# A decoder step with product-key experts: 72 instead of 64 tokens weighed from gathered expert rows, with a third place for the rows and half of each group's rows sent one group ahead

## The chip, the cores and the metric

The kernel runs as one program on one core of a Trainium2 chip. The metric is the device time of one execution in microseconds (us). TensorE (PE) multiplies, VectorE (DVE) and ScalarE (ACT) prepare its operands, GpSimd (POOL) issues the indirect DMAs (gathers and scatters), and SyncE (SP) issues the plain loads. The engines have their own instruction streams and meet at semaphores.

## The reference, cut to what matters

288 tokens (256 of a prompt, 32 of eight samples) go through a mixer stage (short convolution and sparse attention) and then through a product-key expert stage with 128 x 128 = 16384 experts. The change touches only the expert stage:

```
qq = (hx @ wq).reshape(pb, PEER_HEADS, 2, PEER_HALF)
s = jnp.einsum('nhcd,hckd->nhck', qq, sub_keys)
...                      # top 16 of the pair sums for each of 8 heads: 128 experts a token
g = jax.nn.softmax(top, axis=-1)
a = jax.nn.gelu(jnp.einsum('nd,nhkd->nhk', hx, u_tab[eidx]), approximate=False)
w = (g * a).astype(hx.dtype)
return jnp.einsum('nhk,nhkd->nd', w, v_tab[eidx])
```

So every token picks 128 of 16384 experts, and its output is a weighted sum of 128 rows of `v_tab`, each 1024 wide.

## The kernel before, in words

**Dense, in float32 by parts.** The expert stage does not look experts up for most tokens: it multiplies all 16384 rows of both tables with the tokens, and sets the weights of unpicked experts to zero. A table is cut into 128 tiles of 128 x 1024. A tile comes in through a ring of four slots (SP, L534 and L541); ACT writes its rounded part `w_hi` (L974), DVE the rest `w_lo` (L1445), and PE multiplies both.

**U stage** (L2168 and L2173, 128 tiles): 24 matmuls a tile, each with all 288 tokens as moving columns. The activations of the dense tokens stay in SBUF (`rows`), those of the gathered tokens (the last `NE`) are stored to DRAM (`act_kept`, L522).

**Routing.** The gates of the first 128 tokens reach the dense weights through DRAM: POOL scatters them (L607), SP loads them back in 32 pieces of 512 columns into four buffers `gates_in` (L530), DVE multiplies them in (`weighed`). The dense tokens from 128 to `ND` are routed on PE in groups of four (`route`, L2222, four matmuls a group), one group at every second U tile from tile 71. There are `GROUPS = (ND - 128) / 4` of them, 24 before.

**V stage** (`value_tile`, L2248 and L2255, 128 tiles): eight matmuls a tile with `w_hi` and `2 * ND` moving columns (the rounded part and the rest of the weights side by side), then eight with `w_lo` and `ND` columns. The moving operands are made by ACT (L1042) and DVE (L1666).

**Gathered tokens.** For the last `NE` tokens the picked rows of V are fetched: one indirect DMA (L617, issued by POOL) fetches for one token the 128 half rows of 512 values, one on each partition, 256 KB. The tokens go in `EGROUPS` groups of four. A group is a unit of two halves (`weigh_unit`, L2286): a half is four fp32 matmuls with 512 moving columns, each with its own 32 columns of the array, and it needs the four gathered rows of that half and the four tokens' weights (L1719), for which POOL gathers the activations from DRAM (L624). The units stand ahead of the V tiles `UNIT_TILES`, so PE's order is written out: the two halves of a unit, then six or seven tiles, then the next unit. There are two places for rows, one for each half; POOL may fetch into a place when the half before it is done (`rows_used`). POOL's order is written out too: `at_tile(t)` waits until V tile `t - 1` is done, and spreads the issues over the tiles. At V tile `SUM_AT` ACT copies the summed units out of PSUM (L1076), and before tile 126 PE turns them (L2295).

Of the kernel before, what the change touches and what calls it, by code (L numbers as in the profile page):

```python
# [47 lines left out]
NE = 64  # L48
# [3 lines left out]
UNIT_TILES = [13 + 7 * g for g in range(EGROUPS)]  # L52
SUM_AT = UNIT_TILES[-1] + 2
STAGE = 4
# [50 lines left out]
UP0 = 17904  # L105
# [13 lines left out]
assert UP0 + RT["sp"][0] <= AR_ROWS and AR["vset"][0] <= AR_ROWS and RT["ab"][0] + GRP * P == RT["abf"][1] and 4 * ND <= 2 * GRP * P  # L119
assert AR_ROWS + (HOTS + 1) * P + ND - P <= min(UP0 + RT["ab"][0], AR["vset"][1])  # L120
MOVES = 3
assert GATES + D <= AUX and 4 * NT + 4 * ND <= KC * NT - P
assert GATES + 2 * PIECE * P <= AUX and AR_ROWS + 2 * GRP * 512 + 2 * PIECE * P <= AR_STAGE
# [96 lines left out]

def v_tile(t):
    pp, dh = t % HALF, t // HALF
    return pp // 32 * 64 + dh * 32 + pp % 32


def program(nc, A, O):
    with ExitStack() as ctx:
# [20 lines left out]
        e_sums, e_ident = aux[:, GATES:GATES + D], h2_over[:, KC * NT - P:KC * NT]  # L248
# [14 lines left out]
        gates_in += [arena[:, x:x + PIECE * P] for x in (AR_ROWS + 2 * GRP * 512, AR_ROWS + 2 * GRP * 512 + PIECE * P)]  # L263
# [23 lines left out]
        at = AR_ROWS - AR["vset"][0]  # L287
# [3 lines left out]
        g_hi, g_lo = hots[:, HOTS, 0:ND - P], arena[:, AR_ROWS + (HOTS + 1) * P:AR_ROWS + (HOTS + 1) * P + ND - P]  # L291
# [8 lines left out]
        e_rows = [arena[:, AR_ROWS + i * GRP * 512:AR_ROWS + (i + 1) * GRP * 512] for i in range(2)]  # L300
# [255 lines left out]
        def _(pool):  # L556
# [57 lines left out]
            def gather_row(k, q):  # L614

                n = ND + GRP * (k // 2) + q
                pool.indirect_dma_start(e_rows[k % 2][:, 512 * q:512 * q + 512], None, A["v"].rearrange("t p (c f) -> (t p c) f", f=512),  # L617
                                        bass.IndirectOffsetOnAxis(row_list[:, n:n + 1], 0), element_offset=(k % 2) * 32 * P * D)\
                    .then_inc(S[f"v_in{k % 2}"], 16)
# [21 lines left out]
            for n in range(2 * GRP):  # L641
                at_tile(3 + n)
                gather_value(n // GRP, n % GRP)
            for g in range(1, EGROUPS):
                T = UNIT_TILES[g - 1]
                if g >= 2:
                    pool.wait_ge(S["s_weights"], 2 + g - 1)
                for half in range(2):
                    pool.wait_ge(S["rows_used"], 2 * (g - 1) + half + 1)
                    gather_row(2 * g + half, 0)  # L650
                gather_row(2 * g, 1)
                at_tile(T + 1)
                gather_row(2 * g + 1, 1)
                next_value(g, 0)
                at_tile(T + 2)
                gather_row(2 * g, 2)
                next_value(g, 1)
                at_tile(T + 3)
                gather_row(2 * g + 1, 2)
                next_value(g, 2)  # L660
                at_tile(T + 4)
                gather_row(2 * g, 3)
                gather_row(2 * g + 1, 3)
                at_tile(T + 5)
                next_value(g, 3)
# [1064 lines left out]
        def _(pe):  # L1730
# [547 lines left out]
            def weigh_unit(k):  # L2278

                g, half = k // 2, k % 2  # L2280
                pe.wait_ge(S[f"v_in{half}"], 16 * 9 * SETB + 16 * GRP * (g + 1))
                if half == 0:
                    pe.wait_ge(S["s_weights"], 2 + g + 1)
                for q in range(GRP):
                    at = 31 + 32 * (GRP * g + q) - g
                    last = pe.matmul(ps[32 * q:32 * q + 32, 6 + half, :], e_wide[:, at:at + 32], e_rows[half][:, 512 * q:512 * q + 512],  # L2286
                                     start=(g == 0), stop=(g == EGROUPS - 1), skip_group_check=True)
# [152 lines left out]
```

## Time and profile before

| | us |
|---|---|
| three runs | 1204.32, 1205.97, 1201.17 (median 1204.32) |
| profiled execution, its own time | 1203.3 |
| its span in the profile | 1201.6 |
| PE busy | 1170.2 (97%) |
| DVE busy | 848.6 (71%) |
| ACT busy | 624.7 (52%) |
| POOL busy | 574.6 (48%) |
| bytes moved by DMA | 263.67 MB, 219 GB/s over the span |

PE is busy nearly all of the span, at a mean granted clock of 0.99. Busy time of a PE instruction overlaps with the next one's, so the pace of PE is read from the distance between starts, not from the mean duration of an instruction. `PEld` is the load of a matmul's stationary operand, which the profile lists by itself.

### The profile page before, as it was taken

Reading aid. Unit: us, or ns where it says so; the run is one execution under the profiler, and the core shown is the slowest. Engines: PE = TensorE matmul, PEld = TensorE weight load, DVE = VectorE, ACT = ScalarE, POOL = GpSimd, SP = SyncE. Lnnn points to the kernel's source line nnn. Section 1 sums busy time; section 2 is a strip of 40 time slices with the busy share of each in tenths; the row PEclk is TensorE's granted clock in tenths of the full one; section 3 lists DMA queues with packets and bytes.
Section 4 is the critical chain, followed back from the end, with each engine's and each line's share of the span. In section 5 each row is a group of like instructions: output and inputs, shape, how many; then the busy total and the mean of one; then the engine's idle time right before and its main releaser. Section 6 shows DMA issues by size and latency. Waiting matters only on the chain.

```text
span 1201.6 us, 23451 instructions
## 1 busy us (share of the span) xinstructions
PE 1170.2 (97%) x8260; PEld 1080.2 (90%) x8260; DVE 848.6 (71%) x1593; ACT 624.7 (52%) x1209; POOL 574.6 (48%) x525
## 2 busy tenths in 40 slices
PE   7999899979999999999999999999999999999998
PEld 5688899957799999999999999999988988788888
DVE  6536465736587699999967788896966666656665
ACT  5424464523254454554556777765655555555554
POOL 3430324542000088777778776203365656565640
PEclk9999998989999999999999999999999999999999
DMA  8673437866675357677776666689888888889883
GB/s 323 208 225 103 127 94 229 277 211 236 170 275 177 105 176 176 167 171 184 171 186 168 154 165 171 201 247 334 319 286 298 290 297 284 279 275 308 287 293 128
DMA packets 140197, 263.67 MB, mean 219 GB/s; under 512 B 50992, under 2 KB 79728, under 8 KB 139376
## 3 DMA queue, kind: packets, MB, share of 16 engines
q1 hardware_dynamic: 100176, 207.29, 52.7%
q0 software_dynamic: 37184, 51.48, 17.3%
q10 hardware_dynamic: 2720, 3.40, 0.8%
q8 instruction: 66, 1.08, 0.3%
q14 instruction: 51, 0.42, 0.1%
HBM read 246.18 MB, written 20.09 MB: 222 GB/s over the span
## 4 chain that ended last, share of the span: by engine, by line
PE 84%; issue 5%; DMA 2%; POOL 2%; POOLq 2%; DVE 2%; SPq 1%; ACT 1%; ACTq 0%; DVEq 0%
PE ps L2168 27%; PE ps L2248 16%; PE ps L2173 13%; PE ps L2255 9%; PE ps L1735 5%; PE ps L2286 2%; PE ps L1882 2%; PE ps L1755 2%; POOLq L571 1%; DMA arena<-in_v,aux 1%; PE ps L2222 1%; POOL arena L572 1%; PE ps L1851 1%; PE ps L1844 1%; PE ps L1762 1%
## 5 line engine op out<-in xcount | busy, mean ns | idle before, releaser
L974 ACT ACTIVATE w_hi<-ring 128x1024 fp32r<-128x1024 f32 x280 | 296.9, 1060 | 333.0 <-issue 258.2
L1445 DVE TENSOR_TENSOR w_lo<-ring,w_hi 128x1024 fp32r<-128x1024 f32 x271 | 331.2, 1223 | 169.0 <-ACT w_hi L974 167.4
L2168 PE MATMUL ps<-h_hi,w_hi 128*128 128x288 f32 x1088 | 294.6, 299 | 0.5 <-ACT w_hi L974 0.5
L2168 PE MATMUL ps<-h_lo,w_hi 128*128 128x288 f32 x1024 | 277.0, 295 | 0.0
L607 POOL DMA_INDIRECT gates<-arena x128 | 243.9, 1906 | 68.3 <-issue 47.0
L617 POOL DMA_INDIRECT arena<-in_v,aux x128 | 135.2, 1057 | 155.0 <-PE ps L2286 63.4
L2168 PEld LDWEIGHTS ps<-h_hi,w_hi 128*128 128x128 f32 x1088 | 205.1, 188 | 1.2 <-ACT w_hi L974 1.0
L2168 PEld LDWEIGHTS ps<-h_lo,w_hi 128*128 128x128 f32 x1024 | 192.4, 188 | 0.0
L2173 PE MATMUL ps<-h_hi,w_lo 128*128 128x288 f32 x1088 | 167.3, 296 | 0.2 <-DVE w_lo L1445 0.2
L2248 PE MATMUL ps<-h_hi,w_hi 128*128 128x448 f32 x680 | 154.0, 368 | 0.9 <-DVE h_hi L1666 0.5
L2173 PEld LDWEIGHTS ps<-h_hi,w_lo 128*128 128x128 f32 x1088 | 151.7, 188 | 0.5 <-DVE w_lo L1445 0.5
L2248 PEld LDWEIGHTS ps<-h_hi,w_hi 128*128 128x128 f32 x680 | 121.4, 189 | 18.4 <-issue 9.9
L2255 PEld LDWEIGHTS ps<-h_hi,w_lo 128*128 128x128 f32 x680 | 89.1, 191 | 2.4
L2255 PE MATMUL ps<-h_hi,w_lo 128*128 128x224 f32 x680 | 89.1, 273 | 0.0
L624 POOL DMA_INDIRECT arena<-act_kept,aux x64 | 65.0, 1016 | 49.4 <-PE ps L2255 33.2
L597 POOL TENSOR_TENSOR w_lo<-ring,w_hi 128x1024 fp32r<-128x1024 f32 x9 | 24.6, 2731 | 133.1 <-ACT w_hi L974 133.1
L2248 PE MATMUL ps<-mov,w_hi 128*128 128x448 f32 x344 | 77.7, 368 | 0.0
L2248 PEld LDWEIGHTS ps<-mov,w_hi 128*128 128x128 f32 x344 | 61.5, 189 | 8.2 <-issue 4.2
L572 POOL DMA_DIRECT2D arena<-in_cache_slc_v x64 | 34.8, 544 | 61.0 <-issue 61.0
L1666 DVE TENSOR_TENSOR h_hi<-arena,h_hi 128x448 fp32r<-128x448 f32 x85 | 52.5, 618 | 0.6 <-ACT h_hi L1042 0.6
L1042 ACT ACTIVATE h_hi<-arena 128x448 fp32r<-128x448 f32 x85 | 47.7, 562 | 1.0 <-DVE arena L1650 1.0
L1735 PE MATMUL ps<-xT,ring 128*128 128x288 f32 x192 | 47.9, 408 | 0.0
(367 smaller groups left out, 1928.3 us busy)
## 6 DMA issues: line engine op xcount, KB each, us to landing
ring<-in_uT SPq DMA_DIRECT2D x128, 512.0 KB, 3.4
ring<-in_v SPq DMA_DIRECT2D x128, 512.0 KB, 4.5
ring<-in_wout SPq DMA_DIRECT2D x32, 512.0 KB, 4.4
ring<-in_wT SPq DMA_DIRECT2D x28, 512.0 KB, 4.3
gates<-aux SPq DMA_DIRECT2D x32, 256.0 KB, 6.0
ring<-in_wtok SPq DMA_DIRECT2D x8, 512.0 KB, 4.9
arena<-in_cache_slc_v POOLq DMA_DIRECT2D x64, 64.0 KB, 3.9
act_kept<-arena SPq DMA_DIRECT2D x32, 128.0 KB, 3.8
```

Source lines behind the costliest of these rows:

```text
L607: pool.indirect_dma_start(gates, bass.IndirectOffsetOnAxis(rt("gi")[:, P + s:P + s + 1].bitcast(U32), 0), rt("gi")[:, s:s + 1], None, comp ...
L617: pool.indirect_dma_start(e_rows[k % 2][:, 512 * q:512 * q + 512], None, A["v"].rearrange("t p (c f) -> (t p c) f", f=512), bass.IndirectO ...
L624: pool.indirect_dma_start(e_act[:, n:n + 1], None, act_kept, bass.IndirectOffsetOnAxis(act_list[:, ND + n:ND + n + 1], 0))\
L974: act.activation(w_hi[e % 2][:, :], ring[:, (W_O + e) % RING, :], ACT.Copy).then_inc(S["w_high"], 1)
L1042: act.activation(mov_parts[t % MOVES][:, :, 0, :], rows[:, 2 * pp:2 * pp + 2, :], ACT.Copy).then_inc(S["mov_high"], 1)
L1445: dve.tensor_tensor(w_lo[e % 2][:, :], ring[:, (W_O + e) % RING, :], w_hi[e % 2][:, :].bitcast(F32), ALU.subtract)\
L1666: dve.tensor_tensor(mov_parts[t % MOVES][:, :, 1, :], rows[:, 2 * pp:2 * pp + 2, :], mov_parts[t % MOVES][:, :, 0, :].bitcast(F32), ALU.su ...
L1735: last = pe.matmul(ps[:, bank, 0:NT], ring[:, i % RING, at + k * P:at + (k + 1) * P], rhs[:, k, :], start=(k == 0), stop=(k == n - 1))
L2168: last = pe.matmul(ps[:, bank, 0:NT], w_hi[e % 2][:, k * P:(k + 1) * P], mov[:, k, :], start=(k == 0 and mov is mov_hi), stop=False, skip_ ...
L2173: last = pe.matmul(ps[:, bank, 0:NT], w_lo[e % 2][:, k * P:(k + 1) * P], mov_hi[:, k, :], start=False, stop=(k == KC - 1), skip_group_chec ...
L2248: last = pe.matmul(ps[:, VBANK[dh][m], 0:2 * ND], w_hi[e % 2][:, h * 512 + m * P:h * 512 + (m + 1) * P], both[h], start=(t % HALF == 0 and ...
L2255: last = pe.matmul(ps[:, VBANK[dh][m], 0:ND], w_lo[e % 2][:, h * 512 + m * P:h * 512 + (m + 1) * P], both[h][:, 0:ND], start=False, stop=( ...
```

## The change

`NE` goes from 64 to 72, so `ND` from 224 to 216 and `GROUPS` from 24 to 22; there are 18 gathered groups instead of 16. The units stand at V tiles 10, 17, 23, 30, 36, 43, 50, 56, 63, 70, 76, 83, 89, 96, 103, 109, 116, 123 instead of 13, 20, ..., 118, so 11 of the 17 distances are seven tiles and six are six tiles; `SUM_AT` goes from 120 to 125. The four buffers `gates_in` become a third place for gathered rows once all 32 pieces are weighed. Half number `k` (two for each group) uses place `k` for the first two and then `(k - 2) % 3`. Of each group's rows, those of the first half are sent one group earlier than before. Several regions of the arena move; the sums are copied into the arena instead of `aux`.

```diff
-NE = 64
+NE = 72
...
-UNIT_TILES = [13 + 7 * g for g in range(EGROUPS)]
+UNIT_TILES = [10] + [17 + 106 * g // (EGROUPS - 2) for g in range(EGROUPS - 1)]
 SUM_AT = UNIT_TILES[-1] + 2
+PLACES = 3
...
+def row_place(k):
+
+    return k if k < 2 else (k - 2) % PLACES
+
+
+def row_uses(k):
+
+    return len([x for x in range(k + 1) if row_place(x) == row_place(k)])
...
+        e_rows.append(gates_in)
+        e_sums = arena[:, AR_ROWS:AR_ROWS + D]
+        row_sems = [("v_in0", 16 * 9 * SETB), ("v_in1", 16 * 9 * SETB), ("k_in0_0", 16 * 4 * 2)]
...
             for n in range(2 * GRP):
-                at_tile(3 + n)
+                if n >= GRP:
+                    at_tile(3 + n)
                 gather_value(n // GRP, n % GRP)
-            for g in range(1, EGROUPS):
+            def next_row(k, q):
+
+                if k < 2 * EGROUPS:
+                    gather_row(k, q)
+
+            T = UNIT_TILES[0]
+            for half in range(2):
+                pool.wait_ge(S["rows_used"], half + 1)
+                gather_row(2 + half, 0)
+            for q in range(1, GRP):
+                at_tile(T + q)
+                gather_row(2, q)
+                gather_row(3, q)
+            for q in range(GRP):
+                next_value(1, q)
+            pool.wait_ge(S["weighed"], PIECES_IN)
+            for q in range(GRP):
+                at_tile(T + 5 + q)
+                gather_row(4, q)
+            for g in range(2, EGROUPS):
                 T = UNIT_TILES[g - 1]
-                if g >= 2:
-                    pool.wait_ge(S["s_weights"], 2 + g - 1)
-                for half in range(2):
-                    pool.wait_ge(S["rows_used"], 2 * (g - 1) + half + 1)
-                    gather_row(2 * g + half, 0)
-                gather_row(2 * g, 1)
+                pool.wait_ge(S["s_weights"], 2 + g - 1)
+                pool.wait_ge(S["rows_used"], 2 * (g - 1) + 1)
+                gather_row(2 * g + 1, 0)
+                gather_row(2 * g + 1, 1)
                 at_tile(T + 1)
-                gather_row(2 * g + 1, 1)
+                gather_row(2 * g + 1, 2)
                 next_value(g, 0)
                 at_tile(T + 2)
-                gather_row(2 * g, 2)
+                gather_row(2 * g + 1, 3)
                 next_value(g, 1)
+                pool.wait_ge(S["rows_used"], 2 * g)
                 at_tile(T + 3)
-                gather_row(2 * g + 1, 2)
+                next_row(2 * g + 2, 0)
                 next_value(g, 2)
                 at_tile(T + 4)
-                gather_row(2 * g, 3)
-                gather_row(2 * g + 1, 3)
+                next_row(2 * g + 2, 1)
+                next_value(g, 3)
                 at_tile(T + 5)
-                next_value(g, 3)
+                next_row(2 * g + 2, 2)
+                next_row(2 * g + 2, 3)
```

## Rows read from the trace of the kernel before

**Rows 1.** Windows: stretch, its us, busy us by engine, clock, DMA share, GB/s
```profile
810.00:836.00 26.00, 26.00 (x197) 26.00 (x197) 17.15 (x27) 12.94 (x34) 10.29 (x8) 1.00 0.96 345
870.00:1000.00 130.00, 130.00 (x850) 113.89 (x843) 81.45 (x98) 70.11 (x93) 80.12 (x80) 1.00 0.88 292
1000.00:1175.00 175.00, 171.60 (x1111) 148.96 (x1111) 110.13 (x139) 92.83 (x123) 100.01 (x97) 1.00 0.85 285
```
**Rows 2.** Chain of waits, U and V stage: start us, us, engine and line, count
```profile
404.32 7.41 PE ps L2198 x64
...
783.62 2.13 PE ps L2168 x16
...
787.30 2.14 PE ps L2168 x16
...
790.50 2.13 PE ps L2168 x16
...
844.55 1.63 PE ps L2248 x8
846.18 0.88 PE ps L2255 x8
```
**Rows 3.** Groups by line and form: array, moving size, count, busy us, mean ns
```profile
L2248 PE MATMUL ps<-h_hi,w_hi 128*128 128x448 f32 x680 | 154.0, 368 | 0.9 <-DVE h_hi L1666 0.5 <-DVE xT L1697 0.4
L2255 PE MATMUL ps<-h_hi,w_lo 128*128 128x224 f32 x680 | 89.1, 273 | 0.0
...
L2198 PE MATMUL ps<-arena 128*128 128x128 f32 x64 | 7.4, 277 | 0.6 <-DVE arena L1481 0.6
```
**Rows 4.** Timeline of PE's weight loads around a unit: start us, us, idle before
```profile
886.57 1.52 PEld L2248 LDWEIGHTS ps<-h_hi,w_hi 128*128 128x128 f32 x8
...
889.28 0.16 PEld L2286 LDWEIGHTS ps<-arena 128*32 128x32 f32 x8
...
890.17 0.13 PEld L2286 LDWEIGHTS ps<-arena 128*32 128x32 f32 x4 [0.30 <-issue]
891.13 1.52 PEld L2248 LDWEIGHTS ps<-h_hi,w_hi 128*128 128x128 f32 x8 [0.84 <-issue]
...
908.95 0.16 PEld L2286 LDWEIGHTS ps<-arena 128*32 128x32 f32 x8
```
**Rows 5.** The same timeline at three later units, first load and next tile
```profile
1007.24 0.16 PEld L2286 LDWEIGHTS ps<-arena 128*32 128x32 f32 x8
...
1009.90 1.53 PEld L2248 LDWEIGHTS ps<-h_hi,w_hi 128*128 128x128 f32 x8 [0.84 <-issue]
...
1028.40 0.16 PEld L2286 LDWEIGHTS ps<-arena 128*32 128x32 f32 x8
...
1031.88 1.51 PEld L2248 LDWEIGHTS ps<-mov,w_hi 128*128 128x128 f32 x8 [0.84 <-issue]
...
1049.68 0.16 PEld L2286 LDWEIGHTS ps<-arena 128*32 128x32 f32 x8
...
1052.69 1.51 PEld L2248 LDWEIGHTS ps<-h_hi,w_hi 128*128 128x128 f32 x8 [0.84 <-issue]
```
**Rows 6.** Timeline of POOL in the group after 889: first and eleventh issue
```profile
891.15 1.08 POOL L617 DMA_INDIRECT arena<-in_v,aux  x1 [4.49 <-PE ps L2286]
...
904.13 0.95 POOL L617 DMA_INDIRECT arena<-in_v,aux  x1 [0.30 <-issue]
```
**Rows 7.** Landing of the gathered rows, answer for line L617
```profile
DMA to landing us min/median/max: 3.3/5.0/7.3
```
**Rows 8.** Landing of the V tiles in the ring, answer for line L541
```profile
DMA to landing us min/median/max: 3.1/4.5/7.9
```
**Rows 9.** Timeline of DVE: the first unit's weights
```profile
864.96 0.16 DVE L1719 TENSOR_TENSOR arena<-arena,aux 128x4 f32<-128x4 f32 x1
```

**Rows 10.** Timeline of POOL: the first gather of activations
```profile
845.33 1.56 POOL L624 DMA_INDIRECT arena<-act_kept,aux  x1 [22.91 <-PE ps L2255]
```
**Rows 11.** Landing of the gathered activations, answer for line L624
```profile
DMA to landing us min/median/max: 3.1/4.4/5.4
```

## What the change will do to the time: prediction

> **What bounds the kernel now.** I read the page first: PE is busy 97% of the span. A busy PE need not be a bound, so I went to the windows of the last third [rows 1]: PE is busy all 130.00 us of 870 to 1000, but only 171.6 of the 175 us from 1000 to 1175, while DVE (81 of 130) and ACT (70 of 130) have room. So the V stage is paced by PE, with small holes late. Then I took PE's pace from the chain, by starts. A U tile takes 3.20 us (787.30 to 790.50), and one with a routed group behind it 3.68 us (783.62 to 787.30), so a group costs 0.48 us. A V tile takes 1.63 us for its eight matmuls with `w_hi` and 0.88 us for the eight with `w_lo` [rows 2], 2.51 us together. The timeline of the weight loads shows the unit: the first load of the tile ahead starts at 886.57, that of the tile behind at 891.13; 4.56 less a tile is 2.05 us. Unit to unit is 19.67 us (889.28 to 908.95) [rows 4], which is 7 x 2.515 + 2.06, so nothing else lies in it.
>
> Last, the waits. A wait of PE for gathered rows is real only as far as the unit gets longer: it takes 1.85 us undisturbed (889.28 to 891.13) [rows 4]; three units in the slow stretch take 2.66, 3.48 and 3.01 us [rows 5]. They lose 0.81 + 1.63 + 1.16 = 3.6 us. Why they are late is seen on POOL: its twelve issues of a group (eight rows, four activations) run without a pause, 1.30 us apart (891.15 to 904.13 are ten steps), so the last row goes out 14.85 us after the unit began (889.28) [rows 4, 6], and is needed 5.7 us later, at the next unit's second half (19.67 + 0.89 - 14.85; 0.89 is 890.17 less 889.28). A row lands after 5.0 us in the median and 7.3 at most [rows 7]. The margin is 0.7 us, and goes wherever landings or issues are slow.
>
> **The change part by part.** The sum is made against the profiled execution's own 1203.3 us (1.7 us around its span of 1201.6); the median shown is 1.0 us above it.
>
> *Narrower V matmuls with `w_hi`.* 1024 of them (128 tiles by 8) go from 448 to 432 moving columns. By the chain, a matmul takes 1.63/8 = 204 ns at 448 columns and 2.13/16 = 133 ns at 288 [rows 2], so a column costs 71/160 = 0.44 ns. 16 columns are 7.1 ns, times 1024: 7.3 us. Bounds: 6.8 (if a column takes one cycle of the 2.4 GHz that [rows 1] show as granted, 1.00) and 7.5 (204 x 16/448). I take **-7.3**.
>
> *Narrower V matmuls with `w_lo`.* 1024 of them go from 224 to 216 columns, at 0.88/8 = 110 ns each. If they went by columns they would take 224 x 0.44 = 99 ns. And 64 matmuls with 128 columns take 7.41/64 = 116 ns [rows 2, 3], no less than those with 224. So 224 columns already lie on a floor, and eight fewer give nothing. Bounds: 0, and 8 x 0.44 x 1024 = -3.6 us if there is no floor for this form. I take **0**, the value of the nearest row in kind (same array, fewer columns).
>
> The Trainium skill speaks of this in "TensorE: Matmul & The Clock Gate". Its section "Back-to-back issue gap" gives N / 2.4 + 2.5 ns for an isolated matmul and says that weight loads add to this at small N; the trace has 204 ns at 448 where that makes 189, and 110 at 224 where it makes 96. By the plain formula the narrower matmuls would give 6.8 + 3.4 = 10.2 us, an estimate from that page, and against that 7.3 by the rows. It is my third rival, below.
>
> *Two more units.* 2 x 2.05 = **+4.1**. Nothing of it is hidden, PE itself does it. Bounds: 3.7 (the bare 1.85) and 4.2.
>
> *Two routed groups fewer in the U stage.* 2 x 0.48 = **-1.0**. The stage is PE's: the chain there is matmul on matmul. Bounds 0 and -1.0. The moves of tile 118's list-making on DVE to 114 and of the first eight row gathers come before anything waits for them; 0.
>
> *The third place and the rows sent ahead.* Of the rows for the next unit, only the four of the second half go out after the unit begins now, as POOL's 1st, 2nd, 3rd and 5th issue. POOL starts 1.87 us after the unit's first load (891.15 less 889.28), the next two follow in 1.3 us steps, the fifth waits for the second tile behind the unit and goes at 2.05 + 2 x 2.46 + 0.3 = 7.3 us. With six tiles between units (the six short gaps) it is needed at 6 x 2.46 + 2.05 + 0.89 = 17.7 us. That leaves 10.4 us where 5.7 were; with seven tiles 12.9. The slowest landing is 7.3 [rows 7]. The first half's rows have a whole group more. POOL's own work keeps up: twelve issues of 1.3 us after 1.87 end at 17.5, and the next group's start in a short gap is at 16.8 + 1.87 = 18.7. So all of the 3.6 us should go: **-3.6**. Bounds: -3.6 and 0 (the slow stretch lasts whatever the order).
>
> *The first units.* The first unit was at 869.6 (889.28 - 19.67). It moves up by three tiles and by what is saved before it: 869.6 - 3 x 2.515 - 1.0 - 10 x 0.057 = 860.5. Its weights were made 4.65 us ahead (864.96 [rows 9]), so they are due at 855.8. The four gathers of activations that they need no longer wait for tile 3; even if they went no earlier than that wait ended (845.3 [rows 10] less 1.0), they are out by 849.5 and land by 854.9, at 5.4 us [rows 11]. Group 2's second half (half 5) stands behind a queue on POOL: the last row of half 4 waits for the end of tile 17, at 860.5 + 2.05 + 7 x 2.457 + 2.05 + 2.457 = 884.3, and five steps of 1.3 us later, at 890.9, half 5's last row goes out. It is needed at 884.3 + 5 x 2.457 + 0.89 = 897.5: 6.6 us against landings of 5.0 to 7.3. Cost 0 to 0.7 us; I take 0.3.
>
> *The rest.* ACT's copy of the sums is its step 125, PE reads it ahead of tile 126, and ACT's steps run ahead of PE's tiles: 0, at most the 1 us of such a copy. The stored activations grow by an eighth, with eight tiles of cover: 0. The last additions shrink by eight columns: 0.
>
> What is late next: nothing near. V tiles land in the ring after 4.5 us, at most 7.9 [rows 8], against four tiles (9.8 us after the change) less ACT's and DVE's 2.3 us, 7.5; and PE needs the tile only some 3 us later.
>
> Sum: 1203.3 - 7.3 + 0 + 4.1 - 1.0 - 3.6 + 0.3 = 1195.8. It is made against an execution 1.0 us below the median; the waits vary with the run, and taking them away leaves less to vary. I say **1196**.
>
> **The rivals.**
>
> *The slow stretch stays (the change does not do what it says).* If what made rows late near 1000 to 1060 is a lasting lack of supply and not a margin, more places only shift it: POOL gets behind, the queue behind its tile waits grows (activations, then rows of both halves), and the units wait as before. For it: PE is short of 3.4 us in [rows 1] in that stretch alone. Against: a margin of 0.7 us over the median landing explains it, and that margin becomes 5. Time: 1195.8 + 3.6 = 1199.4.
>
> *DMA is the bound (other side).* A group now brings 8 x 0.262 MB of rows and 6.65 x 0.524 MB of tiles, 5.58 MB in 113 x 2.457/17 + 2.05 = 18.4 us: 303 GB/s, against 292 and 285 in the two long windows [rows 1]. If the queues can't sustain more than the 285, a group takes 19.6 us, 1.2 us more, seventeen times: 1195.8 + 20 = 1216. The point from which it decides: the kernel ends slower than before where less than 5.58/(18.4 + 7.5/17) = 296 GB/s is sustained. For it: a DMA share of 0.88. Against: 345 GB/s at a share of 0.96 for 26 us, with PE busy for all of them [rows 1].
>
> *The `w_lo` matmuls do get shorter.* 1195.8 - 3.6 = 1192.2. For it: 110 ns is below the 116 of 128 columns, so the floor is not sharp. Against: a pace by columns would be 99 ns, and the trace has 110.
>
> **How the numbers follow.** Forecast 0.63 (own range 1193.5 to 1198.3); slow stretch stays 0.20 (1198 to 1201); `w_lo` shorter 0.10; DMA the bound 0.07. Range: 1191.5 to 1201.5, which leaves out the DMA case and the ends of the others, some 2 in 10 with the unknowns. 0.5% is about what a measurement of this kernel can tell from no change: 6 us, so faster is below 1198.3 and slower above 1210.3. Faster: 0.60 of the forecast, 0.10, and 0.01 of the slow stretch, 0.71. Slower: 0.05 of the DMA case and 0.01 of mishaps, 0.06. Same: the rest, 0.23.
>
> **What would show it.** In the chain, the eight `w_hi` matmuls of a V tile in 1.57 us and the eight `w_lo` in 0.88; 18 units of 1.85 us each, with distances of 19.3 and 16.8 us; a first unit near 860.5; the end of the U stage 1.0 us earlier; no idle time of PE before L2286 that lengthens a unit, except perhaps at the third; a DMA share near 0.91 and some 303 GB/s from 870 to 1170. Wrong would be: units longer than 1.85 us over the whole stage (DMA), or near 1000 to 1060 alone (slow stretch); `w_lo` in 0.85 us; ACT idle for `ring<-in_v` at many tiles.

## The result, and the profile after

The changed kernel takes **1195.96 us** in the median of 11 runs (1194.02 to 1199.16), the kernel before 1202.55 beside it (1200.07 to 1206.08, 11 runs). The ratio is 0.9941, with a 95% interval of 0.9929 to 0.9953. The prediction was 1196.0.

The profiled execution of the changed kernel is its slowest, 1199.16 us with a span of 1197.5. This matters below: it shows a wait that the faster runs, by their times, had less of. Line numbers moved: the `w_hi` matmuls are L2283, those with `w_lo` L2290, the units L2322; POOL's gathers of rows are L632, those of activations L639.

The chain of waits (start, us, engine and line, count) answers to [rows 2]:
```profile
920.37 1.85 PE ps L2322 x16
922.23 1.76 PE ps L2283 x8
923.98 0.88 PE ps L2290 x8
924.87 1.57 PE ps L2283 x8
...
937.13 1.85 PE ps L2322 x16
```
Eight `w_hi` matmuls take 1.57 us where they took 1.63, the eight with `w_lo` 0.88 as before, and a unit of 16 matmuls 1.85. The first tile behind a unit shows 1.76, and this belongs to the unit's cost: unit to unit is 16.76 us (920.37 to 937.13), less six tiles of 2.453 this is 2.04.

The windows (stretch, its us, busy us of PE, PEld, DVE, ACT and POOL, clock, DMA share, GB/s) answer to [rows 1]:
```profile
870.00:1000.00 130.00, 127.14 (x837) 112.74 (x836) 80.33 (x99) 68.75 (x92) 98.36 (x87) 0.99 0.89 301
1000.00:1170.00 170.00, 169.57 (x1131) 151.88 (x1130) 111.69 (x141) 92.61 (x123) 123.28 (x109) 1.00 0.90 306
```
The hole has changed places. From 1000 on PE is now busy all but 0.4 us, where 3.4 of 175 us were missing. But from 870 to 1000, which was full, 2.9 us are missing, and the clock has fallen to 0.99. The timeline of PE's weight loads shows where (start, us, the idle time before in brackets with what ended it); it answers to [rows 4]:
```profile
860.48 0.16 PEld L2322 LDWEIGHTS ps<-arena 128*32 128x32 f32 x8
...
862.33 1.46 PEld L2283 LDWEIGHTS ps<-h_hi,w_hi 128*128 128x128 f32 x8 [0.84 <-issue]
...
896.45 0.11 PEld L2322 LDWEIGHTS ps<-aux,arena 128*32 128x32 f32 x2
...
900.37 0.16 PEld L2322 LDWEIGHTS ps<-arena 128*32 128x32 f32 x8 [3.76 <-DMA arena<-in_v,aux]
901.87 2.53 PEld L2283 LDWEIGHTS ps<-h_hi,w_hi 128*128 128x128 f32 x8 [1.34 <-issue]
904.41 1.05 PEld L2290 LDWEIGHTS ps<-h_hi,w_lo 128*128 128x128 f32 x8
...
920.30 0.16 PEld L2322 LDWEIGHTS ps<-arena 128*32 128x32 f32 x8
```
The first unit begins at 860.48 and takes 1.85 us. The third begins at 896.45, and its second half can start only at 900.37, when the rows of half 5 are there. The unit takes 5.42 us (901.87 less 896.45) and not 1.85. All other units in the trace take 1.85. Then the tile behind it is slow too, as the windows of 2 us in the same columns show:
```profile
898.00:900.00 2.00, 0.00 (x0) 0.00 (x0) 0.56 (x2) 0.00 (x0) 1.67 (x2) 1.00 0.91 324
900.00:902.00 2.00, 1.63 (x9) 0.29 (x9) 0.00 (x0) 0.00 (x0) 1.58 (x2) 0.70 0.88 330
902.00:904.00 2.00, 2.00 (x6) 1.85 (x7) 0.00 (x0) 0.00 (x0) 1.50 (x2) 0.50 0.70 232
904.00:906.00 2.00, 2.00 (x15) 1.94 (x14) 0.06 (x1) 1.15 (x2) 1.39 (x3) 0.95 0.76 199
```
The granted clock goes from 1.00 to 0.50, which is 2.4 to 1.2 GHz, for 3.4 us after PE had stood still for some 3 us. From the third unit to the fourth it is 23.85 us (896.45 to 920.30), where a gap of seven tiles takes 19.21: 4.64 us are lost. The wait itself is 3.0 of them: the second half stands 0.89 behind the first [rows 4], would have started at 897.34, and started at 900.37. The other 1.6 fall in the stretch at the lower clock: 0.5 in the rest of the unit (1.50 us from 900.37 to 901.87 where 0.96 is usual) and 1.07 in the tile behind it. This execution less the 4.64 is 1194.5, and the fastest of its kernel is 1194.02.

Why the rows were late is seen on POOL (start, us of the issue, idle before it):
```profile
862.48 1.35 POOL L632 DMA_INDIRECT arena<-in_v,aux  x1 [0.30 <-PE ps L2322]
...
884.92 1.68 POOL L632 DMA_INDIRECT arena<-in_v,aux  x1 [0.30 <-issue]
...
892.33 1.63 POOL L632 DMA_INDIRECT arena<-in_v,aux  x1 [0.30 <-issue]
...
919.37 0.95 POOL L632 DMA_INDIRECT arena<-in_v,aux  x1 [0.30 <-issue]
...
922.18 1.06 POOL L632 DMA_INDIRECT arena<-in_v,aux  x1 [1.86 <-PE ps L2322]
```
From 862.48 to 919.37 POOL has no pause beyond its 0.30 us between two issues, and first waits for a unit again at 922.18. Half 5's last row goes out at 892.33, and it is the one that PE waits for, as the chain of waits around the third unit says:
```profile
890.67 1.35 POOL arena L639
...
892.33 8.00 DMA arena<-in_v,aux
900.37 1.57 PE ps L2322 x8
901.94 2.82 PE ps L2283 x8
```
It takes 8.00 us from issue to landing, more than the 7.3 that was the slowest before [rows 7]. The answer on landing for L632 reads:
```profile
DMA to landing us min/median/max: 3.6/5.1/8.0
```
The rows land in the median like before, 5.1 us against 5.0.

### The profile page after: what moved, and what is told of

Its sections match the earlier page's. It is cut to its first block, busy times and chain, and to the rows that moved or that the text cites. A ratio compares the mean times of both kernels' runs of the same rounds, so it can differ in the third digit from the quotient of the medians.

```text
span 1197.5 us, 23519 instructions
## 1 busy us (share of the span) xinstructions
PE 1166.8 (97%) x8284; PEld 1081.9 (90%) x8284; DVE 842.2 (70%) x1585; ACT 619.4 (52%) x1197; POOL 622.7 (52%) x549
## 4 chain that ended last, share of the span: by engine, by line
PE 85%; issue 4%; DMA 2%; POOLq 2%; DVE 2%; SPq 1%; POOL 1%; ACT 1%; ACTq 0%; DVEq 0%
PE ps L2203 27%; PE ps L2283 17%; PE ps L2208 13%; PE ps L2290 9%; PE ps L1770 5%; PE ps L2322 3%; PE ps L1917 2%; POOLq L586 1%; PE ps L1790 1%; POOL arena L587 1%; PE ps L2257 1%; PE ps L1886 1%; PE ps L1879 1%; PE ps L1891 1%; DMA arena<-in_v,aux 1%
## 5 line engine op out<-in xcount | busy, mean ns | idle before, releaser
L632 POOL DMA_INDIRECT arena<-in_v,aux x122 | 139.9, 1147 | 82.7 <-DVE aux L1654 33.1
L2283 PE MATMUL ps<-h_hi,w_hi 128*128 128x432 f32 x680 | 150.0, 362 | 1.0 <-DVE h_hi L1701 0.5
L2283 PEld LDWEIGHTS ps<-h_hi,w_hi 128*128 128x128 f32 x680 | 122.3, 190 | 15.9 <-issue 12.1
L639 POOL DMA_INDIRECT arena<-act_kept,aux x72 | 83.8, 1163 | 64.3 <-DMA act_kept<-arena 29.8
L2290 PEld LDWEIGHTS ps<-h_hi,w_lo 128*128 128x128 f32 x680 | 89.1, 191 | 1.8
L2290 PE MATMUL ps<-h_hi,w_lo 128*128 128x216 f32 x680 | 88.9, 273 | 0.0
L2283 PE MATMUL ps<-mov,w_hi 128*128 128x432 f32 x344 | 75.1, 360 | 0.0
L2283 PEld LDWEIGHTS ps<-mov,w_hi 128*128 128x128 f32 x344 | 61.5, 189 | 5.8 <-issue 4.2
L1701 DVE TENSOR_TENSOR h_hi<-arena,h_hi 128x432 fp32r<-128x432 f32 x85 | 51.8, 611 | 0.6 <-ACT h_hi L1077 0.6
L435 POOL DMA_DIRECT2D arena<-in_cache_cmp_v x32 | 17.2, 537 | 63.3 <-issue 63.3
```

Of the source, the lines that this page charges most:

```text
L632: pool.indirect_dma_start(e_rows[row_place(k)][q], None, A["v"].rearrange("t p (c f) -> (t p c) f", f=512), bass.IndirectOffsetOnAxis(row_ ...
L639: pool.indirect_dma_start(e_act[:, n:n + 1], None, act_kept, bass.IndirectOffsetOnAxis(act_list[:, ND + n:ND + n + 1], 0))\
L1701: dve.tensor_tensor(mov_parts[t % MOVES][:, :, 1, :], rows[:, 2 * pp:2 * pp + 2, :], mov_parts[t % MOVES][:, :, 0, :].bitcast(F32), ALU.su ...
L2283: last = pe.matmul(ps[:, VBANK[dh][m], 0:2 * ND], w_hi[e % 2][:, h * 512 + m * P:h * 512 + (m + 1) * P], both[h], start=(t % HALF == 0 and ...
L2290: last = pe.matmul(ps[:, VBANK[dh][m], 0:ND], w_lo[e % 2][:, h * 512 + m * P:h * 512 + (m + 1) * P], both[h][:, 0:ND], start=False, stop=( ...
```

## The experiments

They ran in three lots of four, each lot on one chip with the kernel before beside it. In the first that kernel took 1204.30 us (1201.47 to 1206.93), in the second 1230.89 (1220.35 to 1236.49), in the third 1233.9 (1226.24 to 1242.28). So times are compared within a lot only.

### First lot: is it the third unit, and what are the parts worth?

**The changed kernel again** (no edit), as the measure for its lot.

> The changed kernel once more, beside the three others of this job. If its one wait (third unit, half 5) comes from the queue on POOL, which has the same length in every execution, the unit at V tile 23 is again longer than 1.85 us, by 1 to 4 us as the landing falls, and the time is 1194 to 1199 us, 5 to 8 us below the kernel before. If the wait was an accident of the one profiled execution, the unit takes 1.85 us and the time is 1194 to 1195.

Measured: 1195.58 us (1193.24 to 1197.78), ratio 0.9927 (0.9911 to 0.9944). The third unit took 3.15 us in this profile, 1.3 too long, and no clock drop came with it: unit to unit 20.52, which is 19.21 + 1.31. So the late rows come back in another execution, with another size, as expected.

**The values of group 2 sent ahead.** The first eight gathers of activations no longer wait for tiles, and the four of group 2 (its values) follow them at once, as soon as their buffer is free; they stood behind the rows of halves 2 and 3, ahead of those of half 4. Half 4's rows may then go a tile earlier. Nothing is computed otherwise.
```diff
             for n in range(2 * GRP):
-                if n >= GRP:
-                    at_tile(3 + n)
                 gather_value(n // GRP, n % GRP)
+            pool.wait_ge(S["s_weights"], 2 + 1)
+            for q in range(GRP):
+                gather_value(2, q)
...
-            for q in range(GRP):
-                next_value(1, q)
...
-                at_tile(T + 5 + q)
+                at_tile(T + 4 + q)
```

> The changed kernel with the four activation gathers of group 2 moved from behind the rows of halves 2 and 3 to the idle stretch of POOL ahead of the first unit, and the rows of half 4 one tile earlier. Theory (the third unit waits for a queue of issues on POOL): the last row of half 5 goes out at about 887 us instead of 892.3, the third unit takes 1.85 us, PE keeps its clock there, and the time is 1194 to 1195, that is 1 to 4 us below the changed kernel beside it. Rival (the DMA queues are short of supply from 862 to 900, where rows and V tiles come together): rows land later as they are sent closer together, 8 us and more, the third unit still waits for 1 us or more or the second one does, and the time is that of the changed kernel, 1196.

Measured: **1193.03 us** (1191.48 to 1193.7), ratio 0.9903 (0.9884 to 0.9922), 2.55 us below the changed kernel beside it. The timeline of weight loads and that of POOL:
```profile
895.63 0.11 PEld L2321 LDWEIGHTS ps<-aux,arena 128*32 128x32 f32 x2
...
897.48 1.46 PEld L2282 LDWEIGHTS ps<-h_hi,w_hi 128*128 128x128 f32 x8 [0.84 <-issue]
```
```profile
886.61 1.63 POOL L632 DMA_INDIRECT arena<-in_v,aux  x1 [0.30 <-issue]
```
Half 5's last row goes out at 886.61, 5.7 us earlier (4.9 as seen from the unit, which itself begins 0.82 us earlier), and the third unit takes 1.85 us (895.63 to 897.48), like all others in the trace. The window of the same columns as above:
```profile
860.00:900.00 40.00, 40.00 (x272) 34.85 (x265) 27.30 (x35) 20.71 (x28) 29.92 (x28) 1.00 0.96 339
```
PE is busy for all 40 us while the DMAs move 339 GB/s. The lateness was POOL's queue and not a lack of supply; what is left is a kernel whose V stage has one stall of 0.7 us in its middle (a distance of 19.92 and not 19.21), and it beats both kernels.

**The third place and the new order alone**, with 64 tokens as before.
```diff
-NE = 72
+NE = 64
...
-UNIT_TILES = [10] + [17 + 106 * g // (EGROUPS - 2) for g in range(EGROUPS - 1)]
+UNIT_TILES = [13 + 7 * g for g in range(EGROUPS)]
...
-UP0 = 17520
+UP0 = 17904
```

> The third place and the new order of the rows alone: 64 tokens in 16 groups at V tiles 13, 20, ..., 118 as in the kernel before. Theory (the third place takes away waits of 0 to 5 us that vary with the run, and nothing else): units of 1.85 us at distances of 19.67 from the fourth on, the lengthened units of the slow stretch gone; 1199.7 us, 2 to 3.5 below the kernel before, and a narrower spread of times. The third unit is needed one tile later than in the changed kernel, so it should not wait, or by under 1 us. Rival (the slow stretch is a lack of supply): lengthened units stay, 1202 to 1204, no difference.

Measured: 1198.17 us (1196.6 to 1199.74), ratio 0.9951 (0.9936 to 0.9966), 6.1 us below the kernel before, where 2 to 3.5 were expected. All units take 1.85 us, and all distances are 19.63 to 19.67 but one of 20.38. That one holds a stall of 0.7 us near 1013 us, where PE waits for DVE (`xT`), and the kernel before has it too (0.68 of its 21.16 us from 1007.24 to 1028.40), so it does not come from the rows. From the first unit to the last it is 295.64 us, against 299.28 in the profile of before: 3.64 less, which is the term of the sum (3.6). The medians differ by 2.5 us more. The profiled execution of before waited 3.6 us at its units; its other runs, up to 1206, may well have waited longer, but no trace of them exists. The window:
```profile
1000.00:1170.00 170.00, 169.57 (x1105) 148.11 (x1104) 108.86 (x136) 92.30 (x122) 98.50 (x93) 1.00 0.85 285
```
It is to be read beside the last of [rows 1]: the same 285 GB/s at the same share of 0.85, but PE has no hole beyond the stall of 0.7 us. What was short there was not the DMAs but the time that the order left them. And from this kernel to the one with the values ahead, 5.1 us are won by eight more tokens, where the sum has 7.7 + 1.0 - 4.1 = 4.6.

**72 tokens with two places and the old order**, the other half of the change.
```diff
-    return k if k < 2 else (k - 2) % PLACES
+    return k % 2
...
-            for g in range(2, EGROUPS):
+            for g in range(1, EGROUPS):
...
-                pool.wait_ge(S["rows_used"], 2 * (g - 1) + 1)
-                gather_row(2 * g + 1, 0)
-                gather_row(2 * g + 1, 1)
+                for half in range(2):
+                    pool.wait_ge(S["rows_used"], 2 * (g - 1) + half + 1)
+                    gather_row(2 * g + half, 0)
+                gather_row(2 * g, 1)
```

> 72 tokens in 18 groups at the new V tiles, but with two places and the order of rows of the kernel before. Theory (what the third place is worth shows only at the closer distance): the last row goes out 14.85 us after a unit's start and is needed at 17.6 us in the six short gaps and at 20.1 in the eleven long ones, against landings of 5.0 in the median. So each short gap costs some 2 us and more as POOL's chain of twelve issues follows the units, the long ones 0 to 1: 12 to 20 us over the wait-free 1194.5, that is 1207 to 1215, slower than the kernel before. Rival (the narrower V matmuls carry the change by themselves and places matter little): 1196 to 1199.

Measured: 1240.93 us (1235.71 to 1243.21), ratio 1.0312 (1.029 to 1.0333): 36.6 us slower than before, far more than I expected. The timeline of weight loads around two units:
```profile
942.35 0.16 PEld L2303 LDWEIGHTS ps<-arena 128*32 128x32 f32 x8 [2.35 <-DMA arena<-in_v,aux]
944.54 0.20 PEld L2303 LDWEIGHTS ps<-arena 128*32 128x32 f32 x8 [2.03 <-DMA arena<-in_v,aux]
...
963.65 0.16 PEld L2303 LDWEIGHTS ps<-arena 128*32 128x32 f32 x8
```
and POOL in the group between them:
```profile
944.81 0.94 POOL L632 DMA_INDIRECT arena<-in_v,aux  x1 [3.49 <-PE ps L2303]
...
959.53 1.63 POOL L632 DMA_INDIRECT arena<-in_v,aux  x1 [0.30 <-issue]
```
and the waits (us in total, times, longest):
```profile
PEld ps L2303 <- DMA arena<-in_v,aux: 46.6, 27, 3.9
```
With two places the chain starts anew with every unit: a half done, twelve issues, the last landing, the next half. It hardly gets shorter where one tile less lies between. The six short gaps take 19.84 us in the mean and the eleven long ones 21.30, 1.5 us apart where a tile is 2.45, and 353.30 together (860.65 to 1213.95). As the short gaps should take 16.76 and the long 19.21, they lose 6 x 3.1 + 11 x 2.1 = 41 us. The expectation had 2 us and more for a short gap and 0 to 1 for a long one: both were too small, and it had not seen that the long gaps are stretched as well. So the 72 tokens, worth 4.6 us, can't be had without the third place and its order: without them they cost some 37, with them the change wins 8.7 in this lot.

### Second lot: what is next to bound it, and the floor of `w_lo`

On this chip the kernel before is 27 us slower than in the first lot.

**The kernel before again** (no edit).

> The kernel before once more, for a second profile. The first one had 3.6 us of lengthened units, all near 1000 to 1060 us, while 64 tokens with the third place (a kernel that only lacks these waits) came out 6.1 us faster in the median. Theory (the margin of 0.7 us is crossed anywhere, and by other amounts in each execution): lengthened units again, at other places than units 8 to 10, 3 to 8 us in all. Rival (a fixed cause near 1000 to 1060): the same three units, 3.6 us in all.

Measured: 1232.21 us, ratio 1.0021 (0.999 to 1.0053). Its V stage takes 325.95 us from the first unit to the last, where the kernel with 64 tokens and the new order took 295.64: 30.3 us are lost, where 3.6 were in the first profile. Its window:
```profile
870.00:1000.00 130.00, 122.32 (x753) 105.31 (x750) 70.99 (x89) 62.75 (x83) 82.94 (x72) 0.95 0.76 260
```
and its largest waits of PE for a DMA:
```profile
PEld ps L2286 <- DMA arena<-in_v,aux: 25.0, 12, 2.6
```
Six of the 16 units are longer, by 0.95 to 2.8 us, and only one of them, the eighth, is among the three of the first profile, so the fixed cause falls; but the loss is far above the 3 to 8 us of the theory. Of the 30.3 us, 12.5 are these longer units. Another 10.2 are waits for the rows of a first half, which come ahead of a unit and do not lengthen it, 3.5 are the tiles behind late units, where the clock falls (0.95 in the window), and 4 are left at other tiles.

Is it the supply of the DMAs? They moved 260 GB/s where 292 were moved before [rows 1], but a kernel that waits moves less, and the rows that PE waited for landed 5.9 to 6.8 us after their issue in the chains around five late units, inside the 3.3 to 7.3 of [rows 7]. What is plainly slower is POOL: the mean of its issues is 82.94/72 = 1.15 us here and 80.12/80 = 1.00 in the same window of [rows 1]. Over the eleven issues up to the last row that is 1.7 us, more than the margin of 0.7. Why the same instructions take longer on this chip no run shows.

**The `w_lo` matmuls with 152 of 216 columns.** The product of `w_lo` is left out for 64 of the dense tokens; all else is the changed kernel. The lines are shortened here.
```diff
-last = pe.matmul(ps[:, VBANK[dh][m], 0:ND], ..., both[h][:, 0:ND],
+last = pe.matmul(ps[:, VBANK[dh][m], 0:ND - 64], ..., both[h][:, 0:ND - 64],
```

> The changed kernel with the w_lo matmuls of the V stage on 152 instead of 216 columns; it leaves out the w_lo part for the last 64 dense tokens. Theory (these matmuls lie on a floor of 110 ns): the eight of a tile still take 0.88 us, a tile 2.45, the time is that of the changed kernel, 1194 to 1199. Rival (a matmul goes by its columns, 0.44 ns each): 64 columns less take 28 ns from each of 1024, 0.66 us for the eight, 1166 to 1170 us.

Measured: 1205.92 us (two runs), ratio 0.9805 (0.9743 to 0.9867), above the 1194 to 1199 expected, and no changed kernel ran beside it. What tells is the pace, which did not hang on the chip: six tiles and an undisturbed unit take 16.76 us in the changed kernel in the result and in the third lot. The chain of waits, in a stretch without a stall:
```profile
938.58 0.85 PE ps L2290 x8
939.42 1.60 PE ps L2283 x8
941.03 0.85 PE ps L2290 x8
```
and the group, by form (array, moving size, count, busy us, mean ns):
```profile
L2290 PE MATMUL ps<-h_hi,w_lo 128*128 128x152 f32 x680 | 86.8, 270 | 1.7 <-issue 1.7
```
From one `w_lo` group to the next it is 2.45 us, and the tile was 2.453 with 216 columns. The eight `w_lo` take 0.03 us less and the eight `w_hi` 0.03 more, and next to nothing is won: six tiles and a unit take 16.74 us and not 16.76. Sixty-four columns fewer would have given 28 ns a matmul by columns, 29 us over the stage (64 x 0.44 x 1024). So 152, 216 and 224 columns lie on one floor of 106 to 110 ns. The Trainium skill ("TensorE: Matmul & The Clock Gate", section "Back-to-back issue gap") gives N/2.4 + 2.5 ns for an isolated matmul, which is 66 ns at 152 columns as an estimate from that page; the same section says that weight loads add at small N, and here, with a weight load for each matmul, the measured 106 to 110 ns decide. The rival that rested on this formula is refuted.

**80 tokens** on top of the values ahead (`NE = 80`, `UP0 = 17200`).

> 80 tokens in 20 groups on top of the kernel with the values ahead (e2, 1193.0): units at 10, 17, 22, 28, 34, 40, 46, 52, 58, 64, 70, 75, 81, ..., 123. Theory (each step of eight tokens gives 0.060 us a V tile and 1.0 us of routing and costs two units): -7.7 - 1.0 + 4.1 = -4.6, that is 1188.4, if POOL and DMA keep up. But the mean distance is 5.89 x 2.39 + 2.04 = 16.1 us, and POOL's twelve issues take 12 x 1.33 to 12 x 1.46 = 16.0 to 17.5 us, so POOL may fall behind by up to 1.4 us a group and eat up the margin of some 5 us after a few groups: then up to 19 x 1.4 - 5 = 22 us more, 1210. Where POOL keeps up but DMA (5.19 MB a group, 322 GB/s) does not, ACT is seen idle for the V tiles in the ring, and not only PE for gathered rows. I expect POOL to fall behind by about half of that: 1195 to 1200, no better than 72 tokens.

Measured: 1226.5 us (12 runs), ratio 0.9968 (0.9943 to 0.9992), 20.6 us more than the kernel above with 72, where 2 to 7 us were expected. The tile got cheaper, 2.409 us, and PE's own sum would be 2.5 us shorter (128 x 0.044 + 1.0 - 4.1). But PE waits. Thirteen of the 20 units in the trace are longer, by 0.7 to 2.6 us and one by 4.8:
```profile
870.00:1000.00 130.00, 123.80 (x809) 107.12 (x807) 73.42 (x94) 64.02 (x85) 99.78 (x85) 1.00 0.83 294
```
It would need 8 x 0.262 + 5.95 x 0.524 = 5.21 MB in 5.95 x 2.409 + 2.04 = 16.4 us, 318 GB/s, and gets 294. That fits a limit of supply, but POOL's twelve issues (the step of back-to-back issues is 1.46 us in the changed kernel, in the mean) fill 17.5 us by themselves, more than such a gap, so the run alone does not say which of the two it is.

**Four more gathers of 512 bytes in each group**, on top of the values ahead. They fetch activations into a spare buffer, add no bytes to speak of, and take POOL's time. The lines are shortened here.
```diff
+            def extra(g, x):
+                n = GRP * g + x
+                pool.indirect_dma_start(staged[0][:, NE + n:NE + n + 1], None, act_kept, ...)
...
                 next_value(g, 0)
+                extra(g, 0)
+                extra(g, 1)
...
                 next_value(g, 2)
+                extra(g, 2)
+                extra(g, 3)
```

> The kernel with the values ahead (e2) with four more gathers of 512 bytes in each group, into columns that nothing reads, so that POOL issues 16 instead of 12 a group and the DMA queues carry almost nothing more. Theory (POOL's issues are the next bound): 16 x 1.33 to 1.46 us = 21.3 to 23.4 us a group where 18.4 are there, units wait from the third group on, 16 x 3 to 5 = 48 to 80 us more: 1240 to 1270. Rival (DMA supply is the next bound, POOL has room): under 3 us more, 1193 to 1196.

Measured: 1276.7 us, ratio 1.038 (1.0316 to 1.0444), 71 us more than the `w_lo` kernel beside it. The windows:
```profile
870.00:1000.00 130.00, 116.79 (x722) 99.26 (x721) 68.21 (x84) 60.36 (x79) 100.06 (x87) 0.97 0.73 255
1000.00:1170.00 170.00, 137.03 (x799) 114.29 (x799) 76.90 (x101) 65.55 (x86) 127.05 (x113) 0.92 0.67 221
```
The DMA share falls to 0.67 while PE stands still: here it is not the bytes, it is the instruction stream of POOL. Its 200 issues in the two windows take (100.06 + 127.05)/200 = 1.14 us, 1.44 with the pause of 0.30. Sixteen of them are 23.0 us, and the mean distance of two units is 23.31 (396.25/17). With 80 tokens, twelve issues of 99.78/85 + 0.30 = 1.47 us are 17.7, and the mean distance is 18.33 (348.18/19): POOL's stream fills nearly all of it there too. With 72 tokens and 1.46 us, twelve issues are 17.5 us, and POOL has 1.7 us of room in a long gap and is 0.8 over in a short one. So POOL's stream is the next bound of the changed kernel, and 80 tokens go past it.

How it reaches PE is only half seen. Of the 83.6 us that the V stage takes more than with the values ahead (312.65), 21 are longer units; most of the rest is lost at tiles, at waits whose end the trace puts down to `issue` or `remote`, so what held those tiles stays open. The extra gathers also bring small packets to the queues, and no run separates these from the time of the issues.

### Third lot: the same on one more chip

**Before, after, values ahead, 80 tokens**, without new edits.

> The kernel before once more, since in the last job (all kernels) the kernel before took 1231 us, 27 more than in the two jobs ahead of it. Theory (its margin of 0.7 us is crossed at other units in each execution): if the time is near 1204 again, 3 to 8 us of lengthened units in the profile, not all near 1000 to 1060; if it is near 1231, more than half of the units are late as in e5. Rival (a fixed cause near 1000 to 1060): the same three units as in the first profile and 3.6 us.

> The changed kernel, as the base for the two beside it. Near 1204 us for the kernel before: 1195.5, with one late unit, the third. Near 1231: about 1206 as e6 (whose w_lo matmuls took the same time), since its margin of 5 us absorbs what the kernel before can't.

> The kernel of e2 again: 2 to 3 us below the changed kernel beside it (1193), the third unit 1.85 us.

> The kernel of e7 again, 80 tokens. In the last job it took 1226.5 with the units late from the fourth on, some 20 us behind e6. Theory (POOL can't issue twelve gathers in 16.1 us, and that does not hang on the chip): most units late by 1 to 3 us again and 8 to 25 us over the kernel with 72 tokens beside it, 1201 to 1218. Rival (only the slow supply of the last job): near 1188.4, units of 1.85 us.

| | us | ratio, 95% |
|---|---|---|
| before | 1231.91 (1227.71 to 1242.4) | 0.9995 (0.9956 to 1.0034) |
| after | 1210.45 (1206.35 to 1212.74) | 0.9808 (0.9768 to 0.9848) |
| values ahead | 1208.3 (1207.52 to 1209.57) | 0.9791 (0.9752 to 0.9831) |
| 80 tokens | 1231.78 (1227.87 to 1234.99) | 0.998 (0.9955 to 1.0006) |

Windows of the first two, before and after:
```profile
870.00:1000.00 130.00, 120.80 (x774) 104.08 (x777) 75.74 (x93) 64.63 (x86) 83.42 (x72) 0.99 0.80 268
1000.00:1170.00 170.00, 160.64 (x997) 137.52 (x990) 95.85 (x122) 81.52 (x106) 108.22 (x94) 0.96 0.78 263
```
```profile
870.00:1000.00 130.00, 125.84 (x811) 109.36 (x811) 75.94 (x94) 67.27 (x88) 96.35 (x84) 0.99 0.87 294
1000.00:1170.00 170.00, 165.96 (x1097) 146.76 (x1096) 106.62 (x137) 90.39 (x119) 128.04 (x108) 1.00 0.86 295
```
The change is worth 2% here and 0.6 to 0.7% in the result and in the first lot. Against the kernels of the first lot that had no late unit (64 tokens with the new order 295.64 us from the first unit to the last, values ahead 312.65), the kernel before loses 29.7 us in its V stage and the changed kernel 13.9.

In the kernel before, seven of the 16 units are longer, not more than half as expected, and that makes 11.3 of the 29.7 us. The length of a unit does not show a wait for its first half, which comes ahead of it:
```profile
951.23 1.06 PEld L2255 LDWEIGHTS ps<-h_hi,w_lo 128*128 128x128 f32 x8
954.88 0.16 PEld L2286 LDWEIGHTS ps<-arena 128*32 128x32 f32 x8 [2.59 <-DMA arena<-in_v,aux]
```
From the last loads for `w_lo` to the unit it is 3.65 us, where 1.17 is usual. Such waits make another 9.7 us. POOL in the group ahead of this unit, and the chain to the row that came last for it:
```profile
934.65 1.16 POOL L617 DMA_INDIRECT arena<-in_v,aux  x1 [2.19 <-PE ps L2286]
...
950.67 1.64 POOL L617 DMA_INDIRECT arena<-in_v,aux  x1 [0.30 <-issue]
```
```profile
950.67 6.56 DMA arena<-in_v,aux
```
The last row goes out 17.9 us after the unit ahead began (932.78), with slower issues and a pause of 1.56 us for a tile in between, where it was 14.85 in [rows 6], and lands 6.56 us later, no slower than in [rows 7]. So the margin went on POOL's side. The tiles behind late units, at the lower clock, take 3.8 us more, and 4.8 are left at other tiles.

In the changed kernel 4.5 us are longer units, no first half is late, 1.5 are tiles behind a late unit, and 7.9 are other tiles. So the order takes away what late rows cost, 24.9 us down to 6.0, which is the mechanism of the first chip with a larger price. The waits at other tiles do not get fewer, in one trace of each. The values ahead remove the late third unit here too (4.33 us to 1.85) and win 2.15 us in the median, 2 to 3 expected; two later units are longer by up to 1.0 us, and what else is left are tiles, as at this one, where the weight load waits for ACT, and ACT's step had waited in turn:
```profile
1069.56 2.66 PEld L2282 LDWEIGHTS ps<-h_hi,w_hi 128*128 128x128 f32 x8 [1.76 <-ACT w_hi L1008]
```
```profile
1068.45 1.06 ACT L1008 ACTIVATE w_hi<-ring 128x1024 fp32r<-128x1024 f32 x1 [2.40 <-remote]
```
Eighty tokens are 23.5 us behind 72 with the same code. The third chip is as slow as the second, so 80 tokens never ran on one like the first, and the rival (the slow chip alone) is not settled by a run; against it, twelve issues at the 1.46 us of the first chip would be 17.5 us in a gap of 16.4. A part of the theory fell: only five of the 20 units are longer by more than 0.4 us, and of some 45 us lost against 113 x 2.409 + 19 x 2.04 = 311 only 8.6 are in the length of units. POOL is busy or in its pauses of 0.30 for 126.9 of the 130 us from 870 on. That is POOL's bound once more, and as with the extra gathers most of the loss shows at tiles, which is not explained.

## Why the prediction was right, point by point

**`w_hi`, -7.3.** Right in kind, 0.4 short. A tile went from 1.630 + 0.883 to 1.570 + 0.883 us by starts, 0.060 us less, times 128 is 7.7, just beyond the upper bound of 7.5.

**`w_lo`, 0.** Right, and shown by the kernel with 152 columns.

**Two units, +4.1.** Right: 2 x 2.04, undisturbed.

**Routed groups, -1.0.** The first `w_hi` matmul of the V stage starts at 835.11, in the profile before at 836.10, 0.99 us earlier. Right.

**Third place and rows ahead, -3.6.** Right in the profiles: no late unit from the fourth on. By the run with 64 tokens the order alone takes 3.64 us off the V stage in the traces, and 6.1 off the medians. The 3.6 were read from one execution, and the medians are further apart. One step of the working was too kind: POOL was to keep up in every gap, with twelve issues of 1.3 us. They take 17.5 us at 1.46, so it is behind by 0.8 us in a short gap and makes it up in the long ones; the new margin had room for that.

**The first units, +0.3.** This is the mis-sized term. The working had the queue and the place right (the third unit, half 5's last row) and each number a little too kind. It was to go out at 890.9 and went at 892.33. Of these 1.4 us, 0.6 are that the queue reached half 4's last row at 884.92 and not at 884.3. The rest is the step: the 1.3 us was that of before, and in a queue without a pause it is 1.46 in the mean (1.48 in these five), with issues of 0.95 us and others of 1.34 to 2.00. It was needed at 897.5 and was at 897.34. It was to land within 7.3 us and took 8.0. To the 0.7 us that the term had as its upper end come 1.4 + 0.2 + 0.7, which is the wait of 3.0 us; and the lower clock adds 1.6, which the term had no place for. Measured: 4.6 in the profile, 1.3 in the profile of the first lot, 2.55 between the medians with and without.

**The sum by measured terms**, for the profiled executions: 1203.3 - 7.7 + 4.1 - 1.0 - 4.2 + 4.6 + 0.7 = 1199.8, against 1199.16. The 4.2 are all that the V stage of before lost against 15 free distances of 19.67 (3.6 at units, 0.6 elsewhere), 0.7 is the stall in the middle of the stage (a distance of 19.91 and not 19.21), which is in the 0.6 of before as well and so no cost of the change; the 0.6 us left are within the rounding of 17 distances. In the medians, the larger worth of the order pays for the larger price of the third unit, and this is why 1196 came out so closely: two errors of some 2 us, of opposite signs. That the sum was right to 2 us is the working's; that it hit 1195.96 is luck.

**The rivals.** *The slow stretch stays* fell: from 1000 on PE is busy 169.57 of 170 us, with 306 GB/s. *DMA the bound* fell on this chip, at the 303 GB/s forecast (301 and 306 measured); on the third chip 294 and 295 GB/s were moved, just below the 296 named as its point, and yet the change won more. The rate moved is no measure of what can be sustained: the share was 0.87 and 0.86 there, and in the kernel before on that chip the row above landed as in [rows 7], while POOL's issues were slower. Whether a lack of supply has a part in the tiles that wait is open. The rival's step that below 296 GB/s the change turns into a loss was wrong in any case: it took the kernel before as undisturbed. *`w_lo` shorter* fell.

## What to carry to other kernels

When buffers are freed by the consumer and refilled by one issuing engine, the length of the refill chain (free, issues, landing) sets the period, and work taken out between two uses wins little: draw it up with a margin for the slowest landing, and a third buffer pays where two leave the chain closed. Look for waits ahead of the consumer as well as inside it: on the slower chips some 10 of 25 us that late rows cost stood ahead of a unit and did not lengthen it. Re-cut the start of such a pipeline as carefully as its steady state: the one late unit left was the third, where a queue meets a cold start, and four small gathers sent ahead took it away. Before taking work off the columns of a matmul, find out by one narrower form whether its pace is on a floor.

## What the runs showed of the hardware that was not expected

- fp32r matmuls with a weight load each took 106 to 110 ns with 152, 216 and 224 moving columns alike, and 196 ns (1.57/8) with 432.
- After PE had stood still for some 3 us the granted clock was 0.50 for 3.4 us and then back at 1.00. The stop of 1.4 us in a unit of the kernel before (PE busy 2.59 of the 4 us from 1028) did not lower it. That one late operand cost 1.6 us beyond its wait. In the third lot's changed kernel a stop of 2.3 us at the third unit was followed by 3.4 us at 0.50 as well.
- POOL's issues of an indirect DMA of 128 rows take 0.95 us with 0.30 between, but 14 of the 40 from 862.48 to 919.37 in the profile after take 1.34 to 2.00; the mean step without a longer pause was 1.33 us in the V stage of the kernel before and 1.45 in that of the one after.
- The same kernel took 1204, 1231 and 1234 us on three chips. In the same stretch of its V stage POOL's issues took 1.15 us (82.94/72) and 1.16 (83.42/72) in the mean on the two slower ones, and 1.00 (80.12/80) in the first profile; 260, 268 and 292 GB/s were moved. What makes the difference is not known.
